# Vectors of the first modulation and norm in PSUM, the factor's steps between its rows, and shifted buffers, in a two-layer hybrid kernel on one core

## What is computed

```python
c_act = jax.nn.silu(c)
mod = jnp.dot(c_act, w_ada[l]) + b_ada[l]
sh1, sc1, ga1, sh2, sc2, ga2 = [m[:, None, :] for m in jnp.split(mod, 6, axis=-1)]
xn = rms_norm(h, g_mix[l]) * (1.0 + sc1) + sh1
proj = jnp.dot(xn, w_in[l]) + b_in[l]
q, k, v, qi, ki, wi, xr, yr, gate_a, gate_b = jnp.split(proj, cuts, axis=-1)
attn = dsa_attention(...)                       # top-k selection by score, then softmax
rnn = rg_lru(causal_dwconv(xr, ...), ..., lru_lambda[l]) * jax.nn.gelu(yr)
merged = sigmoid(gate_a) * dot(attn, w_o_attn) + sigmoid(gate_b) * dot(rnn, w_o_rnn)
h = h + ga1 * jnp.dot(merged, w_out[l])
xn = rms_norm(h, g_ffn[l]) * (1.0 + sc2) + sh2
h = h + ga2 * dot(silu(gte) * val, w_down[l])   # val, gte: two halves of a short convolution of xn @ w_up
```

## Time and profile before

| | us |
|---|---|
| median of 3 runs | 1821.93 |
| lowest and highest | 1821.19, 1822.06 |
| the profiled execution | 1819.59 |
| its span, first to last instruction | 1817.8 |

### The profile page before, as it was taken

One profiled execution on the slowest core, in us unless ns is written; L12 is line 12 of the kernel. 1 busy time (PEld: TensorE's weight loads), 2 busy tenths in 40 slices (PEclk: granted clock), 3 DMA queues, 4 the chain that ended last, 5 costly groups with the idle time before them and its releaser, 6 DMA issues.

```text
span 1817.8 us, 33586 instructions
## 1 busy us (share of the span) xinstructions
PE 1767.7 (97%) x11448; PEld 1564.5 (86%) x11448; DVE 1071.7 (59%) x1677; ACT 526.8 (29%) x775; POOL 1474.3 (81%) x2245
## 2 busy tenths in 40 slices
PE   5899999999999999999999999999999999999997
PEld 2567776677899999888899999999999999999886
DVE  6958988845566677522656655665665455555102
ACT  3235664420221111100543443443343211111001
POOL 1977896568999999999677877876886999989885
PEclk8799999999999999999999999999999999999999
DMA  9743232322322322333122222222221322223332
GB/s 366 271 146 112 87 95 88 116 81 93 93 93 92 92 90 87 101 104 102 60 77 75 82 70 70 82 72 70 81 82 60 103 93 92 92 92 93 104 104 93
DMA packets 55328, 184.42 MB, mean 101 GB/s; under 512 B 6673, under 2 KB 9905, under 8 KB 55250
## 3 DMA queue, kind: packets, MB, share of 16 engines
q1 hardware_dynamic: 52018, 177.53, 30.0%
q10 hardware_dynamic: 3232, 5.77, 0.9%
HBM read 178.56 MB, written 4.72 MB: 101 GB/s over the span
## 4 chain that ended last, share of the span: by engine, by line
PE 89%; DVE 4%; POOL 2%; DMA 1%; issue 1%; ACT 1%; SPq 1%; DVEq 1%; ACTq 0%; POOLq 0%
PE gp L401 27%; PE gp L402 27%; PE gp L403 27%; PE A L729 2%; POOL Wlo L392 1%; DMA raw<-units 1%; PE A L527 1%; DMA AW<-ada 1%; PE A L560 1%; PE gp L586 1%; POOL probe L388 1%; PE A L776 0%; PE A L578 0%; SPq L328 0%; PE A L725 0%
## 5 line engine op out<-in xcount | busy, mean ns | idle before, releaser
L392 POOL TENSOR_TENSOR Wlo<-raw,Whi 128x256 fp32r<-128x256 f32 x1120 | 969.7, 886 | 46.7
L401 PE MATMUL gp<-XNhi,Whi 128*128 128x264 f32 (+3 forms) x2736 | 847.8, 310 | 24.7 <-POOL Wlo L392 18.6
L402 PE MATMUL gp<-XNlo,Whi 128*128 128x264 f32 (+3 forms) x2736 | 835.8, 305 | 0.0
L403 PE MATMUL gp<-XNhi,Wlo 128*128 128x264 f32 (+3 forms) x2736 | 833.2, 305 | 0.0
L401 PEld LDWEIGHTS gp<-XNhi,Whi 128*128 128x128 f32 x2736 | 516.2, 189 | 64.2 <-POOL Wlo L392 19.2
L402 PEld LDWEIGHTS gp<-XNlo,Whi 128*128 128x128 f32 x2736 | 516.9, 189 | 24.2 <-issue 2.2
L403 PEld LDWEIGHTS gp<-XNhi,Wlo 128*128 128x128 f32 x2736 | 516.1, 189 | 23.4
L388 POOL TENSOR_TENSOR probe<-raw 1x1 f32<-1x1 f32 x560 | 182.2, 325 | 277.5 <-PE gp L403 213.6
L389 POOL TENSOR_SCALAR Whi<-raw 128x512 fp32r<-128x512 f32 x560 | 348.0, 621 | 0.0
L401 PE MATMUL gp<-AChi,Whi 128*128 128x512 f32 (+1 forms) x374 | 142.8, 382 | 0.0
L403 PE MATMUL gp<-AChi,Wlo 128*128 128x512 f32 (+1 forms) x374 | 142.6, 381 | 0.0
(11 more groups left out here) (316 smaller groups left out, 2276.5 us busy)
## 6 DMA issues: line engine op xcount, KB each, us to landing
raw<-units SPq DMA_DIRECT2D x280, 512.0 KB, 3.5
AW<-ada SPq DMA_DIRECT2D x40, 512.0 KB, 7.3
AWL<-ada SPq DMA_DIRECT2D x8, 512.0 KB, 3.6
bias_rows<-RB ACTq DMA_DIRECT2D x1, 2560.0 KB, 19.3
H<-xT SPq DMA_DIRECT2D x1, 2048.0 KB, 8.8
BIAS<-bias_rows ACTq DMA_DIRECT2D x1, 2048.0 KB, 8.6
out<-H SPq DMA_DIRECT2D x8, 256.0 KB, 2.2
WG<-gatew ACTq DMA_DIRECT2D x8, 128.0 KB, 2.0
```

The lines of the kernel that those rows point to most:

```text
L392: ins = pool.tensor_tensor(lo[:, c:c + UNIT // 4], src[:, c:c + UNIT // 4], hi[:, c:c + UNIT // 4].bitcast(F32), ALU.subtract)
L401: pe.matmul(dst, Whi[s][:, k, :], rhi, start=start, stop=False)
L402: pe.matmul(dst, Whi[s][:, k, :], rlo, start=False, stop=False)
L403: return pe.matmul(dst, Wlo[s][:, k, :], rhi, start=False, stop=stop)
```

## The change

- `CS` is still written, and then copied by ScalarE into `CSP`, which is `A67`; the 40 reduces of `modulation` read `CSP`. `modulate` goes on reading `CS`.
- The first norm's scale goes to `RSTP` (`A45`, first half), its scaled chunks `nt` to three half buffers of PSUM (`NTP`). Its outputs are `XAhi` and `XAlo`: the same memory as `XNhi` and `XNlo`, read as dense rows of 512 columns from its start. All 44 units of the first layer that multiply the first norm's output read these.
- The first norm's statistics are summed in `A45` instead of `A67`. The scores use other halves of PSUM (`SCP`), and the fourth score waits for `WI`.
- ScalarE takes the inverse root of the extra rows right behind the norm's own, and the three exponentials right behind the norm's last chunk. In front of the third chunk VectorE waits for `MRS`.
- VectorE's steps for the lower bound and the factor are cut into pieces (`bound_ratio`, `factor_begin`, `factor_terms`, `factor_end`) and stand between the reduces, the last piece behind score 17. Tiles 36 to 39 are reduced two and two behind scores 5 and 11.
- `AHEAD` is changed: six tiles instead of four behind unit 3, and fewer later.
- 224 bytes for each partition, `fill`, are allocated ahead of the buffers of the later frames, which all move by that much: `nt`, `RG8`, `RNhi`, `AThi`, `MGhi`, `AChi`, `M2hi` and what follows them.

```diff
-AHEAD = [0, 4, 4, 4, 3, 4, 3, 2]
+AHEAD = [0, 4, 4, 6, 3, 3, 3, 1]
@@ buffers
+        XAhi, XAlo = [x[:, :, :].rearrange("p k n -> p (k n)")[:, 0:KC * S].rearrange("p (k n) -> p k n", k=KC)
+                      for x in (XNhi, XNlo)]
+        sb("fill", [P, 56])
+        CSP = A67[:, 0:D]
+        RSTP = A45[:, 0:S]
+        NTP = (gp[1][:, 512:1024], A45[:, 512:1024], gp[0][:, 512:1024])
+        SCP = (A45[:, 0:512], A45[:, 512:1024], gp[1][:, 512:1024], gp[0][:, 512:1024])
@@ TensorE
+                pe.wait_ge(rb_copied, 1)
-                    pe.matmul(A67[:, 0:S], mean, sq[:, k % 2, 0:S], start=(k == 0), stop=(k == KC - 1)).then_inc(stat_mm, 1)
+                    pe.matmul(RSTP, mean, sq[:, k % 2, 0:S], start=(k == 0), stop=(k == KC - 1)).then_inc(stat_mm, 1)
+                if n == 3:
+                    pe.wait_ge(wi_ready, 1)
-                unit(u, u % 2, gp[u % 2], S, XNhi, XNlo, META, range(KC), last=KC - 1).then_inc(unit_done, 1)
+                unit(u, u % 2, gp[u % 2], S, XAhi, XAlo, 0, range(KC), last=KC - 1).then_inc(unit_done, 1)
@@ ScalarE
-            act.activation(CS[:, :], A67[:, 0:D], ACT.Silu).then_inc(silu_c, 1)
+            act.activation(CS[:, :], CSP, ACT.Silu)
+            act.drain().then_inc(cs_saved, 1)
+            act.activation(CSP, CS[:, :], ACT.Copy).then_inc(silu_c, 1)
+                elif m == 0:
+                    act.wait_ge(stat_mm, KC)
+                    inverse_root(RSTP, RSTP, EPSC, rstd_ready)
+                    act.wait_ge(meta_mm, 1)
+                    inverse_root(MRS[:, :], gp[0][:, 512:512 + META], EPSC, meta_rstd)
@@ VectorE, norm_split
+                dve.wait_ge(meta_rstd, 1)
+                    hi, lo = [x[:, k, c0:c0 + n] for x in (XNhi, XNlo)] if m else [x[:, k, :] for x in (XAhi, XAlo)]
+                    dve.scalar_tensor_tensor(lo, nt[:, k % 3, 0:n] if m else NTP[k % 3], scale_bias(m, k)[1],
+                                             hi.bitcast(F32), ALU.add, ALU.subtract).then_inc(xn_ready, 1)
@@ VectorE, modulation
-                    dve.tensor_tensor_reduce(w[:, :], w[:, :], CS[:, :], 1.0, 0.0, ALU.mult, ALU.add,
+                    dve.tensor_tensor_reduce(w[:, :], w[:, :], CSP, 1.0, 0.0, ALU.mult, ALU.add,
@@ VectorE, order
-            modulation(ADA_FIRST, ADA_MID)
+            modulation(ADA_FIRST, ADA_FIRST + 8)
+            bound_ratio()
+            modulation(ADA_FIRST + 8, ADA_FIRST + 11)
+            factor_begin()
+            modulation(ADA_FIRST + 11, ADA_FIRST + 17)
+            factor_terms(13, 11, 9, 7)
+            modulation(ADA_FIRST + 17, ADA_FIRST + 20)
+            factor_terms(5, 3, 1)
@@ VectorE, behind score n
+                if n in (5, 11):
+                    c = ADA_MID - 4 + (n // 6) * 2
+                    modulation(c, c + 2)
+                if n == 17:
+                    factor_end()
```

## The result

| | before | after |
|---|---|---|
| median, us | 1821.56 (4 runs, 1821.01 to 1822.06) | 1789.38 (4 runs, 1789.32 to 1789.57) |
| the profiled execution | 1819.59 | 1789.43 |
| its span | 1817.8 | 1787.5 |

The account below looks back on a forecast made before the run. TensorE, busy for 97% of the span, was taken as the bound. Gains of 16.9 us up to the first gates and 6.8 us from rows sum to 23.7: 1795.9 us for the profiled run, median 1798.2, range 1791 to 1808.

Parts of the forecast that it names:

- TensorE's clock in the first pair: Units 0 and 1: clock 0.50, 0.43 us a matmul, until 53.6 us; the last 18 matmuls at full clock, 4.2 us.
- Step 1: Conditioning vector in PSUM: a reduce takes 1.15 us, a GpSimd half 2.3; units 2 to 6 then take 27.8 us.
- Step 2: First norm's scale and chunks in PSUM: last chunk ready at 49.9 us, unit 2 starting at 57.8 against 62.46.
- Unit 4's slack: Weights of unit 4 land near 64 us, split by GpSimd at 66.4, needed at 68.9: slack 2.5 us.
- rival B: The loads become late: units 4 to 7 come every 7 us, costing 5.6 us, 1803.8 us; chance 0.15.
- Step 3: Factor's steps moved ahead of and between scores: the 3.0 us wait on `rnn_xc` goes, gain 16.9 us by the first gates.
- For `WI` 1.0 us: TensorE's wait for `WI` at its fourth score, charged at 1.0 us with bounds 0 and 4.
- Step 4: Dense rows and moved buffers: 3.3 ns off each 512-column matmul, 40 ns off each `XA` unit; 6.8 us in all.
- The upper bound of 10 us: Upper bound on the rows' gain, if the shortest single gap of chunk 3 became the rule.
- C: The change doesn't do what it says and the VectorE and GpSimd turns stay: 1817.0 us; chance 0.03.
- A: The start of a row doesn't matter, shorter chunks 3 and 7 having another cause: 1805.0 us; chance 0.18.
- D: Rows all at multiples of 512 collide in TensorE's reads: slower, 1830.4 us at 10 ns a matmul; chance 0.02.

Follow-up runs that it names:

- e6: The kernel before with `CSP` alone (copy, the 40 reduces reading it, and the PSUM halves that it forces): 1810.61 us, ratio 0.9949.
- e7: The changed kernel with the first norm's scale and scaled chunks back in SBUF, the reduces staying on PSUM: 1794.49 us, ratio 0.9859.
- e9: The changed kernel with all the lower bound's and factor's steps in one row behind score 23: 1795.23 us, ratio 0.986.
- e1: The kernel before with the 224 bytes of `fill` and nothing else: 1811.98 us, ratio 0.9952.
- e3: The changed kernel with the first norm's output again in rows of 528 columns, the fill staying: 1792.14 us, ratio 0.9841.
- e10: The changed kernel with the old list `AHEAD`: 1788.40 us, ratio 0.9822.
- e5: The changed kernel with the 40 reduces reading `CS` in SBUF again: 1803.51 us, ratio 0.9907.
- e8: The changed kernel with rows of `XN` and `M2` 576 columns apart and each stage's first column chosen, cut still in halves: 1791.11 us, ratio 0.9836.
- e13: The changed kernel with the factor's steps behind the scores, but the four of `bound_ratio` kept between the reduces: 1792.12 us, ratio 0.9844.

## Why the prediction was right and wrong

**What failed.** The change did what it was to do in every part, and the forecast was 8.8 us too high. The steps that failed are two sizes: the price of a row's start, put at 3.3 ns for a matmul where it is 6.6 (3.8 us), and TensorE's clock in the first pair, kept at 0.50 where the change itself raised it (2.4 us). Another 2.3 us are the step from the profiled run to the median.

**The parts, measured one by one, nearly add up.** By the medians: reduces' source -10.2 (e6), norm in PSUM -5.1 (e7), factor between rows -5.9 (e9), fill -9.0 (e1), dense rows -2.8 (e3), new `AHEAD` +1.0 (e10). Sum -32.0; measured -32.2. That they meet so closely is partly luck. Some parts were added to the kernel before and some taken from the changed one, and for the reduces the two ways differ: with e5's 14.1 in place of e6's 10.2 the sum is -35.9. The factor's 5.9 is its price in the changed kernel, where the clock falls behind the wait; in the kernel before the wait cost 3.0. That the parts are near to adding up fits: TensorE was 97% busy and stays the bound.

**Step 1, reduces: right.** 1.14 us apart (57.61 to 58.75 was that alone; now also beside GpSimd), a half in 2.3 us. Unit 2 to transposes was to take 27.9 us and takes 28.04; two small errors cancel there by luck, 0.6 us for five dense units at 5.44 instead of 5.56, and the 0.5 us wait for unit 4. A reduce from PSUM takes 1.208 us and one from SBUF 1.22, so the fixed cost that the Trainium skill ("VectorE: DVE Perf Modes", TRN2 errata) gives a PSUM source is not seen here.

**Step 2, norm: mechanism right, the clock mis-sized by 2.4 us.** Last chunk ready at 48.5 + 0.75 = 49.3, forecast 49.9. But unit 2 starts at 55.42, not 57.8. The step that failed is "the two steps with six matmuls end at 48.4 + 12 x 0.43": it kept the 0.50 of the earlier trace rows for a stretch in which the change itself makes TensorE nearly busy. Every chunk from the fourth on (43.98 us) runs at full clock. e7 supports it: with the chunks up to 2.3 us apart the clock stays low to 56 us.

**Unit 4's slack was 0.5 us short, not 2.5 long.** It was to land near 64 and be split at 66.4, with TensorE at 68.9; GpSimd began it at 64.51 and TensorE asked at 66.4, since step 2 came earlier than forecast. The landing was forecast well; the one who needs it was not. That is rival B at 0.5 us instead of 5.6: the transfers held 413 GB/s in 66 to 71 us, not 297.

**Step 3, factor: right, but for 1 us.** The wait on `rnn_xc` is gone. For `WI` 1.0 us was charged and none came: it was scaled at 84.57, and TensorE's fourth score found it done. The 3.0 us for the wait itself were right, since the clock behind it was at 1.00 in the kernel before; e9 shows that in the changed kernel such a wait costs half as much again through the clock.

**Step 4, rows: mechanism right, size low by 3.8 us.** Forecast 6.8; the trace has 9.2 behind the gates and some 1.4 ahead of them (an estimate: twelve units at 0.12 us). The term that failed is 3.3 ns for a matmul: it is 6.6. The 0.690 came from chunk 3 of the earlier trace rows, which stands between two chunks that start elsewhere. Where all rows start alike it is 0.680; e8 shows the same in the 528-column stage, where a chunk's pace in a mixed sequence did not carry over. The upper bound of 10 us named this case, and the forecast gave it no weight. One small term had the wrong sign: the 132 matmuls of 256 columns lose 3.3 ns each. By the prediction's own counts 6.6 ns everywhere would be 9.7 - 0.4 + 5.0 = 14.3 us; it came to 10.6, mainly because the dense rows brought 2.8 us (e3) and not 5.

Together: 2.4 + 1.0 - 0.5 + 3.8 = 6.7, of the 6.5 missed. **Rivals:** A fell with e1 (the Trainium skill's 16-byte lines, "Advanced Engine Details and Errata", section "Memory Cachelines", would have had e1 change nothing; the measured 8 to 9 us decide); B at a tenth of its size; C did not occur, and e5 is its picture in part; D is wrong for 512 columns, and for 256 it has the right sign, at 3.3 ns, though 128 bytes past a multiple of 256 is as slow.

## What to carry to other kernels

When an edit makes an engine's feed denser, its clock in the stretch is part of the edit: take it from a row in which the engine is fed as it will be, not from the row it replaces. When a row of the trace is used as a price, ask whether its neighbours are alike; a gap between starts in a mixed sequence is an average. Row starts are worth a look at the address sum in any kernel bound by long float32r matmuls, and have to be tried for each width anew.

## What the runs showed of the hardware

- A float32r matmul of 512 columns on `AC` or `MG` is followed by the next after 226.7 ns if its rows start at a multiple of 256 bytes, after 232.4 (`AC`) and 233.4 (`MG`) at 128 bytes past one, and after 233.3 at 32. On `RN`, moved alike, it is 229.6 instead of 233.2; why not 226.7 is open. One of 256 columns: 120.0 ns at a multiple of 256, 119.8 at 128 past, 116.7 at 32 past.
- VectorE instructions with one input of two in PSUM, or with PSUM output, are as short as from SBUF beside an idle GpSimd (0.743 and 0.754 us for 512 columns, 1.208 for the reduce), and don't hold GpSimd up; with both inputs in SBUF they take 1.2 and 1.75 us beside it.
- Behind waits of 2.8, 3.9 and 4.6 us (e13, e9, e5) TensorE's granted clock was at 0.5 within 0.5 us of the next matmul and stayed there for 3 to 5 us of full work; behind 3.0 us in the kernel before it didn't fall.
- The first product started at 39.76, 38.50 and 39.52 us in three kernels that differ only in the amount of fill (224, 96 and 480 bytes), with the transfers saturated at 412 to 415 GB/s in all three. There is one trace of each, so whether chance or the buffers' places move the start is not shown.
